# Stick-breaking attention with the queries on the partitions, 512-column products in the up halves, and the last four down halves one token tile at a time

## What is computed

```python
for start in range(0, seq, SB_BLOCK):          # SB_BLOCK = 128
    end = start + SB_BLOCK
    z = jnp.einsum("bhqd,bhkd->bhqk", qb, kb).astype(jnp.float32) * scale
    past = s_idx < t_idx
    log_beta = jax.nn.log_sigmoid(z)
    log_1mb = jnp.where(past, jax.nn.log_sigmoid(-z), 0.0)
    between = lax.cumsum(log_1mb, axis=3, reverse=True) - log_1mb
    a = jnp.where(past, jnp.exp(log_beta + between), 0.0)
    outs.append(jnp.einsum("bhqk,bhkd->bhqd", a.astype(vb.dtype), vb))
...
x = x + jnp.square(jax.nn.relu(h2 @ w_up[l])) @ w_down[l]
```

## Time and profile before

| | |
|---|---|
| time of the kernel before, median of 3 runs | 1226.34 us (1226.33 to 1226.4) |
| the profiled execution, its own time | 1226.2 us |
| its span in the trace | 1224.4 us |
| mean granted clock of TensorE | 0.998 |
| PE busy | 1204.7 us, 98% |
| DVE busy | 772.5 us, 63% |
| ACT busy | 609.4 us, 50% |
| DMA | 219.25 MB, mean 179 GB/s |

### The profile page before, as it was taken

The page is one execution under the profiler, slowest core; times in us unless marked ns, Lnnn a source line. Parts: engine busy times, 40 slices in busy tenths (PEclk is TensorE's granted clock), DMA queues, the critical chain, the costliest instruction groups (busy, mean ns, idle before and its releaser), DMA issues.

```text
span 1224.4 us, 17707 instructions
## 1 busy us (share of the span) xinstructions
PE 1204.7 (98%) x7176; PEld 1053.1 (86%) x7176; DVE 772.5 (63%) x883; ACT 609.4 (50%) x711; POOL 3.5 (0%) x10
## 2 busy tenths in 40 slices
PE   7999999999999999999999999999999999999997
PEld 6999987888888799899888789999988878899995
DVE  5676966474555665555458687555575868755555
ACT  6565555555444454444257545444435654544441
POOL 0000000000000000000000000000000000000000
PEclk9999999999999999999999999999999999999999
DMA  7654243543655355554364445545436444564540
GB/s 255 207 210 166 104 173 139 205 172 138 218 207 183 126 206 207 176 202 173 135 236 178 147 173 206 207 172 206 171 137 242 168 150 172 199 214 172 206 171 34
DMA packets 34490, 219.25 MB, mean 179 GB/s; under 512 B 4080, under 2 KB 6144, under 8 KB 9088
## 3 DMA queue, kind: packets, MB, share of 16 engines
q1 hardware_dynamic: 33792, 216.31, 49.6%
q0 software_dynamic: 640, 2.11, 0.5%
HBM read 217.34 MB, written 1.06 MB: 178 GB/s over the span
## 4 chain that ended last, share of the span: by engine, by line
PE 92%; DVE 6%; ACT 1%; issue 1%; DMA 0%; SPq 0%; DVEq 0%; ACTq 0%
PE gps L1440 33%; PE gps L1479 9%; PE gps L1487 9%; PE gps L1480 9%; PE aps L1479 7%; PE aps L1480 7%; PE aps L1487 7%; DVE w_lo L788 1%; PE aps L1602 1%; PE aps L1505 1%; DVE rs L919 1%; ACT w_hi L341 1%; DVE B L929 1%; PE aps L1641 1%; DVE B L870 1%
## 5 line engine op out<-in xcount | busy, mean ns | idle before, releaser
L788 DVE TENSOR_TENSOR w_lo<-raw,w_hi 128x2048 fp32r<-128x2048 f32 x194 | 444.2, 2291 | 260.4 <-ACT w_hi L341 259.9
L341 ACT ACTIVATE w_hi<-raw 128x2048 fp32r<-128x2048 f32 x194 | 370.5, 1911 | 208.0 <-PE aps L1487 104.1
L1440 PE MATMUL gps<-R_hi,w_hi 128*128 128x256 f32 x672 | 175.8, 283 | 0.0
L1440 PE MATMUL gps<-R_hi,w_lo 128*128 128x256 f32 x672 | 175.7, 283 | 0.0
L1479 PE MATMUL aps<-w_hi,Q_hi 128*128 128x512 f32 x416 | 162.2, 390 | 0.5 <-DVE Q_lo L1201 0.5
L1480 PE MATMUL aps<-w_lo,Q_hi 128*128 128x512 f32 x416 | 162.2, 390 | 0.0
L1440 PE MATMUL gps<-R_lo,w_hi 128*128 128x256 f32 x672 | 135.4, 283 | 0.0
L1440 PEld LDWEIGHTS gps<-R_hi,w_lo 128*128 128x128 f32 x672 | 128.9, 192 | 0.8
L1440 PEld LDWEIGHTS gps<-R_hi,w_hi 128*128 128x128 f32 x672 | 128.8, 192 | 0.8
L1479 PE MATMUL gps<-w_hi,H_hi 128*128 128x512 f32 x288 | 114.8, 399 | 0.0
L1480 PE MATMUL gps<-w_lo,H_hi 128*128 128x512 f32 x288 | 112.5, 390 | 0.0
(11 more groups left out here) (241 smaller groups left out, 1670.6 us busy)
## 6 DMA issues: line engine op xcount, KB each, us to landing
raw<-w SPq DMA_DIRECT2D x194, 1024.0 KB, 4.8
B<-rows SPq DMA_DIRECT2D x4, 1024.0 KB, 5.6
raw<-w SPq DMA_DIRECT2D x8, 256.0 KB, 6.0
B<-turns POOLq DMA_DIRECT2D x4, 512.0 KB, 7.7
B<-x_t SPq DMA_DIRECT2D x4, 256.0 KB, 5.4
B<-mem_t SPq DMA_DIRECT2D x1, 1024.0 KB, 8.9
B<-x SPq DMA_DIRECT2D x1, 1024.0 KB, 6.8
out<-B SPq DMA_DIRECT2D x4, 256.0 KB, 2.0
```

The lines of the kernel that those rows point to most:

```text
L341: act.activation(w_hi[:, ring(l), :], raw[:, raw_slot(l), :], ACT.Copy)\
L788: dve.tensor_tensor(w_lo[:, ring(l), :], raw[:, raw_slot(l), :], w_hi[:, ring(l), :].bitcast(F32), ALU.subtract)\
L1440: return pe.matmul(gps[:, bank_, nt * T:(nt + 1) * T], w[:, r, c:c + P], op[:, k, :], start=start, stop=stop, skip_group_check=True)
```

## The change

**Attention.** The queries are on the partitions now. The scores come as 128 and 256 columns for each head, the keys moving. The masks are gone: `past` holds 0 or -3.0e38 and is added to the two diagonal blocks once (`sb_masked`), after ACT has copied the block off the diagonal (`sb_full`). The sums over later keys are a scan on DVE along the free dimension, from the right, which `keep` resets between the blocks of one head. What goes to PE instead are six transposes of 128 columns for each pair (`sb_transpose`), behind the odd halves 13 to 27, and ACT copies the result (`sb_copy`) for the value products. The Exp stands at the odd step of its own pair and no longer one step later; the argument (`sb_arg`) is made by DVE at the odd step, behind the split of the even one.

**Up halves.** `R_hi` and `R_lo` are one tensor `R_both`. The product of w_hi with both is one instruction of 512 columns, w_lo with R_hi stays at 256 columns: 32 products for a half and not 48. High and low sums lie side by side in a bank, two banks for a half; ACT copies the low sums, DVE adds the high ones, then takes relu and square in one instruction.

**Last four down halves.** In the last MLP alone the halves 28 to 31 are multiplied with token tile 0 first, all four, and then with tile 1.

```diff
@@ up halves, PE
+            def rows_wide(h0, l, a):
+                r = ring(l)
+                pe.wait_ge(s["lo_ready"], h0 + (l + 1))
+                for nt in range(2):
+                    b = wide_bank(a, nt)
+                    for k in range(KT):
+                        c = k * 256 + nt * P
+                        pe.matmul(b.rearrange("p (i t) -> p i t", i=2), w_hi[:, r, c:c + P], R_both[:, :, k, :],
+                                  start=(k == 0), stop=False, skip_group_check=True)
+                        ins = pe.matmul(b[:, 0:T], w_lo[:, r, c:c + P], R_hi[:, k, :],
+                                        start=False, stop=(k == KT - 1), skip_group_check=True)
+                ins.then_inc(s["gemm_done"], 1)
...
-                        pe.wait_ge(s["ffn_relu"], free_count + a)
-                        rows_first(h, l + a, (2 * par_ + a + 1) % 4, R_hi, R_lo)
+                        pe.wait_ge(s["ffn_relu"], free_count + a)
+                        rows_wide(h, l + a, a)
...
-                    up(hf, l0 + 6, 0, uf + 1)
+                    up(hf, l0 + 6, uf + 3)
...
-                    up(hf, l0 + 10, 1, uf + 3)
+                    up(hf, l0 + 10, uf + 5)
@@ up halves, ACT
-                act.activation(staged[:, a, :], up_bank(par_, a), ACT.Relu)\
-                   .then_inc(s["ffn_relu"], 1)
-                act.wait_ge(s["ffn_relu"], uu + 1)
+                for nt in range(2):
+                    act.activation(staged[:, a, nt * T:(nt + 1) * T], wide_bank(a, nt)[:, T:2 * T], ACT.Copy)\
+                       .then_inc(s["up_low"], 1)
+                act.wait_ge(s["ffn_sq"], uu + 1)
                 t0 = 4 * par_ + 2 * a
-                act.activation(Q_hi[:, t0:t0 + 2, :], two(staged[:, a, :]), ACT.Square)\
+                act.activation(Q_hi[:, t0:t0 + 2, :], two(hid_s[:, a, :]), ACT.Copy)\
@@ up halves, DVE
+                for nt in range(2):
+                    t = staged[:, a, nt * T:(nt + 1) * T]
+                    dve.wait_ge(s["up_low"], 2 * uu + (nt - 3 - 4 * n))
+                    ins = dve.tensor_tensor(t, t, wide_bank(a, nt)[:, 0:T], ALU.add)
+                ins.then_inc(s["ffn_relu"], 1)
                 dve.wait_ge(s["ffn_relu"], uu + 1)
-                dve.tensor_tensor(hid_s[:, a, :], staged[:, a, :], staged[:, a, :], ALU.mult)\
+                dve.scalar_tensor_tensor(hid_s[:, a, :], staged[:, a, :], 0.0, staged[:, a, :], ALU.max, ALU.mult)\
@@ last four down halves, PE
+                for m in range(2):
+                    for par_ in range(2):
+                        pe.wait_ge(s["hidden"], ub + 14 + 2 * par_)
+                        for a in range(2):
+                            l = l0 + 28 + 2 * par_ + a
+                            pe.wait_ge(s["lo_ready"], h0 + (l + 1))
+                            ins = tokens_part(l, acc(m, a), m, par_, Q_hi, Q_lo, stop=(par_ == 1))
+                            if m:
+                                ins.then_inc(s["gemm_done"], 1)
+                            elif par_:
+                                ins.then_inc(s["acc_ready"], 1)
@@ attention, ACT
-                if SB0 <= h <= SB0 + 18 and h % 2 == 0:
+                if SB0 <= h <= SB0 + 18:
                     t = (h - SB0) // 2
...
+                    if h % 2 == 0:
+                        if t >= 2:
+                            sb_out(t - 2)
+                        if t < SB_PAIRS:
+                            sb_softplus(t)
+                    elif t < SB_PAIRS:
+                        if t >= 1:
+                            sb_copy(t - 1)
+                        sb_exp(t)
@@ attention, DVE
+                dve.wait_ge(s["sb_sp"], i + 1)
+                dve.scalar_tensor_tensor(soft[:, :, :], b, 0.0, soft[:, :, :], ALU.max, ALU.add)\
+                   .then_inc(s["sb_sum"], 1)
+                dve.wait_ge(s["sb_sum"], i + 1)
+                for hh in range(2):
+                    ins = dve.tensor_tensor_scan(soft[:, hh, ::-1], keep[:, ::-1], soft[:, hh, ::-1], 0.0,
+                                                 ALU.mult, ALU.add)
+                ins.then_inc(s["sb_suffix"], 1)
+                dve.wait_ge(s["sb_suffix"], i + 1)
+                dve.tensor_tensor(b, b, soft[:, :, :], ALU.subtract).then_inc(s["sb_arg"], 1)
@@ attention, PE
-                    pe.matmul(aps[:, 2 + hh, 0:384], gt, soft[:, hh, :], start=True, stop=False)
-                    ins = pe.matmul(aps[:, 2 + hh, 128:256], ones, soft[:, hh, 256:384],
-                                    start=False, stop=True)
+                    for j in range(3):
+                        ins = pe.transpose(aps[:, 2 + hh, j * P:(j + 1) * P],
+                                           spb[:, i % 2, hh, j * P:(j + 1) * P], ident)
```

More of the change, by code:

```diff
@@ L440, in up_relu @@
                     act.wait_ge(s["ffn_sq"], ub + m - 1)
-                act.activation(staged[:, m, :], up_bank(0, m), ACT.Relu).then_inc(s["ffn_relu"], 1)
+                act.activation(staged[:, m, :], up_bank(m), ACT.Relu).then_inc(s["ffn_relu"], 1)
             def up_hi(n, ub, m):
                 act.wait_ge(s["up_tr"], 2 * n + m + 1)
-                act.activation(Q_hi[:, 0:4, m * P:(m + 1) * P], four(up_bank(0, m)), ACT.Copy)\
+                act.activation(Q_hi[:, 0:4, m * P:(m + 1) * P], four(turned(0, m)), ACT.Copy)\
                    .then_inc(s["ffn_hi"], 1)
@@ L499, in sb_exp, with sb_copy @@
                 act.activation(b, b, ACT.Exp).then_inc(s["sb_e"], 1)
+            def sb_copy(i):
+                act.wait_ge(s["sb_t"], i + 1)
+                if i >= 1:
+                    act.wait_ge(s["sb_o"], i)
+                act.activation(sb_pt, aps[:, 2:4, 0:384], ACT.Copy).then_inc(s["sb_pt"], 1)
             def head_squares(n):
@@ L1014, in ffn @@
                     split_gates(n)
-            diag2 = past.unsqueeze(1).to_broadcast([P, 2, P])
-            def mask_diagonals(b, done):
-                for hh in range(2):
-                    t = b[:, hh, :].rearrange("p (c n) -> p c n", c=3)[:, 0:3:2, :]
-                    ins = dve.tensor_tensor(t, t, diag2, ALU.mult)
-                ins.then_inc(done, 1)
             def sb_out(i):
@@ new lines, in ffn @@
+                down(h0 + 16, l0 + 8, 1, ub + 12)
+                up(h0 + 16, l0 + 10, ub + 13)
+                for m in range(2):
[9 more added lines that the diff above has]
+                                ins.then_inc(s["acc_ready"], 1)
@@ L1623, in turn_heads @@
                 if n == 0:
-                    pe.wait_ge(s["sb_lb"], SB_PAIRS)
+                    pe.wait_ge(s["sb_past"], SB_PAIRS)
                 else:
@@ L1763, in _ @@
                         sb_scores(t)
-                    if 1 <= t <= SB_PAIRS:
-                        sb_between(t - 1)
+                if SB0 + 3 <= h <= SB0 + 17 and h % 2:
+                    sb_transpose((h - SB0 - 3) // 2)
                 if h - 2 in heads_ends:
```

143 lines of the change are left out of this document (70 added, 73 removed).

## The result

The changed kernel takes 1236.53 us (median of 4 runs, 1235.52 to 1237.12), the kernel before 1226.37 us beside it. The ratio is 1.008, with a 95% interval of 1.0068 to 1.0092: it is slower by about 10 us, and the forecast of 1228.2 with its range of 1221 to 1234 missed it. The profiled execution took 1237.12 us, its span is 1235.3 us against 1224.4 before, a difference of 10.9.

A forecast was written before the change was run, and what follows sets the result against it. PE's list of instructions was taken to bound the kernel. From the profiled 1226.2 us, attention +11.9, up halves -9.0 and tail -1.0 gave 1228.1, or 1228.2 with the median 0.14 higher; range 1221 to 1234.

The forecast's parts named there:

- Attention, +11.9: Attention stage: ACT and DVE wait for each other in laps of about 16.5 us, PE wants 13.84; 11.9 us more.
- the heads' transposes: End of attention, after half 27 ends at 210.0: first heads' transposes wait for the head scale, reached at 212.9.
- the wait for the head scale: After half 27: DVE reaches the head scale at 212.9, behind argument and split of the last lap; PE waits from 210.0.
- Up halves, -9.0: Up halves of three MLPs: 672 fewer matmuls, 0.0133 us each beside their columns, 9.0 us less on PE.
- the top of its bounds: Up halves: gain between 0, if the new product costs as much as two matmuls, and 9.0 us.
- The fourth rival: Up halves: 512-column products gain only 1.7 us, as 13 ns stay with weight load or two-part operand; 1235.5 us, 7%.
- I price it at nothing: MLP: new wait for `ffn_relu` before an up half, covered by two down halves, 10.9 us; 2 to 4 without cover.
- some 18 us in a period of 22.0: MLP, ACT and DVE: two up-with-split chains of about 6.7 us and two more splits, against PE's period of 22.0.
- The wait that the forecast named, before an up half: MLP: PE's wait for `ffn_relu`, one pair later than before; priced at nothing, 2 to 4 us if not covered.
- Tail, -1.0: Last four down halves: tile 0 first lets residual (1,1) start at 1215.8 instead of 1216.79; 1.0 us less.
- only 0.6 us from one: Last down halves: split of half 31 needed after 8.2 us, there 7.6 us after the up pair; so no wait.
- the laps are hidden: Rival, attention: ACT and DVE laps are hidden and PE sets the pace; 1206.0 us, 1206.1 with the median's difference, 8%.

The follow-up runs named there:

- In groups: Kernel before with the up halves' change alone, in each half of a bank eight 512-column products first, then eight 256-column ones, not in turn: 1222.91 us, ratio 0.9972.
- the fastest kernel: Changed kernel with attention splits before the pair's functions, MLP loop splits inside the up step, 512-column up products before 256-column ones: 1210.3 us, ratio 0.9869.
- the run with the splits first: Changed kernel, but in the attention stage ACT splits before Abs, Exp, Ln in even steps and before the last Exp in odd ones: 1216.39 us, ratio 0.9915.

## Why the prediction was wrong

By the marks of the table the miss is 8.8 us: 4.8 by the price of a product (9.0 less three times the first MLP's 1.41), 2.1 in the second MLP, 1.7 in the third with the tail, 0.3 between them.

- **Attention, +11.9: right** in mechanism up to pair 5, and in the sum partly by luck. Values were forecast at 117.8, 185.0, 203.7 and 219.2 and came at 117.88, 184.80, 205.88 and 219.34; a pair's two scans were forecast at 1.88 and took 1.81. Wrong was the place of the last loss: not the heads' transposes waited, but the product behind the evacuation and squares of step 25, by 4.98 us, and the products after it ran at half the clock. So pair 6 came 2.2 us later than forecast, and the wait for the head scale, which was to cost about as much behind it, did not come. These two errors cancel; the match of the last values to 0.1 us is luck.
- **Up halves, -9.0: the step that failed first is the price of a product.** It took the pitch of equal products (0.12 and 0.226) for the pitch of a mixed sequence, though no row showed one. Its caution was for something else, the two pieces of the operand, which cost nothing, and it took the top of its bounds. In turn they take 0.355 a pair, so 672 pairs save 3.4 to 3.7 us. In groups they take 0.350. The fourth rival, 1235.5 with a gain of 1.7 us, came within 1 us of the measured time, but its reason is not what the runs show. The Trainium skill, page "TensorE: Matmul & The Clock Gate", section "Wait — 56ns, not 53.3ns?", gives about 2.5 ns as the fixed cost of a warm product; by that each removed product would give an estimated 2.5 ns. The first MLP has 224 removed products and no new wait of PE. With the up halves' change alone it became 1.28 us shorter in turn and 2.50 in groups, 5.7 and 11.2 ns for each. In groups a half takes 5.57 to 5.58 us in the fastest kernel against 5.76 in the earlier trace rows, which is 11 to 12 ns too. This case agrees with the page in neither.
- **"I price it at nothing": the second step that failed.** The forecast added up the busy time of ACT and DVE for four halves ("some 18 us in a period of 22.0") and saw slack. It left the transfers out of that ring. With them the ring is 21.67 us, of which ACT waits 5.5 for transfers and 5.9 for DVE's squares. The wait that the forecast named, before an up half, did not come: the ring never makes PE wait in the middle of an MLP, but the lag from the start of the MLP is still there at its end, where it shows as the wait of 1.76 us before the second MLP's end norm and as waits in the tail. The second MLP lost 0.65 us where 1.4 by the measured pitch and 3.0 by the forecast were to be won.
- **Tail, -1.0: right as a term, but eaten by waits.** From the start of the last product to the end of the span it is 8.04 us, against 9.04 with the up halves alone, so the 1.0 us came. The forecast saw the order "only 0.6 us from one", a wait, by a chain that started on time. In the changed kernel it did not: the last but one split started at 1203.24 and the last at 1209.43, and PE waited for the hidden block and for the split:

```profile
1208.65 1.07 PE L1517 MATMUL aps<-w_hi,Q_lo 128*128 128x512 f32 x4
1210.30 0.50 PE L1509 MATMUL aps<-w_hi,Q_hi 128*128 128x512 f32 x1 [0.59 <-DVE Q_lo L994]
...
1212.25 1.07 PE L1517 MATMUL aps<-w_hi,Q_lo 128*128 128x512 f32 x4
1213.71 0.50 PE L1509 MATMUL aps<-w_hi,Q_hi 128*128 128x512 f32 x1 [0.39 <-DVE w_lo L809]
```

  The list counts 0.98 us, but by the distance of starts the waits cost more. Four products in a row take 0.91 us; here the next one starts after 1.65 and 1.46, and the first product behind each wait takes 0.34 instead of 0.23. That is 1.5 us, which eats the gain: against the up halves alone the tail's order costs 0.6 us here instead of winning 0.9.
- **The range** counted the up halves' 9.0 as nearly sure and gave the ring no case of its own. The rival "the laps are hidden" (1206) was judged rightly for this order; one changed order later it was nearly true.

## What to carry to other kernels

Where two engines with fixed lists hand work to each other, follow each ring all the way round, transfers and their buffers included, and compare its length with the bound engine's period: a sum of busy times can say "slack" where the ring has none, and a saving on the bound engine shows only as far as the ring lets it. Put work that waits for nobody (here the split) into the gap where an engine would wait for the other's answer, on both engines at once. One engine's list alone, reordered, can close a new ring through a buffer.

## What the runs showed of the hardware

A 512-column product behind a 256-column one starts its follower 0.235 us later instead of 0.226 to 0.230, and the 256-column one behind it starts the next after 0.117 instead of 0.120; a down half that follows an up half shows it too, with its first products 0.23 us apart and the later ones 0.226 to 0.228. Why was not settled.

Waits of PE cost clock as well as time. Busy time of PE, granted clock and DMA of stretches of the changed kernel, and the products behind its wait of 4.98 us:

```profile
76.00:140.00 64.00, 59.92 (x491) 0.97 0.42 148
140.00:200.00 60.00, 50.03 (x353) 0.96 0.35 123
200.00:206.00 6.00, 5.41 (x14) 0.53 0.36 126
```

```profile
201.61 0.63 PE L1509 MATMUL gps<-w_hi,R_both 128*128 128x512 f32 x1
202.04 0.63 PE L1510 MATMUL gps<-w_lo,R_both 128*128 128x512 f32 x1
```

Products of 512 columns are 0.427 us apart there, the lower level of 1.2 GHz, for some 5 us. In the run with the splits first, where PE does not wait, the clock is 1.00 in both of the first two stretches. An estimate from these traces: the stretch up to the first MLP's norm is 12.05 us longer, PE's own work in it some 8.8 shorter (eight pairs at 14.0 for 15.1), and the listed waits are 14.7, so some 6 us are what the waits cost beyond their idle time, in the clock and the restart. The scan on 128 partitions, backwards and in place, takes 944 ns for 384 columns in the median of 16, just the 0.94 that the earlier trace rows gave for 8 partitions.
